# FFN up's first four steps on layer norm 1's scaled input, with mean and deviation applied to their products

## The reference

```
z = x @ w_in                                   # four token mixers and the merge gates
merged = sum_k sigmoid(gate_k) * (branch_k @ w_branch[k])
x = layer_norm(alpha * x + merged @ w_out, ln1_g, ln1_b)
gate_ff, up_ff = split(x @ w_ffn_up, 2)        # 2 x 5632 columns
x = layer_norm(alpha * x + (silu(gate_ff) * up_ff) @ w_ffn_down, ln2_g, ln2_b)

layer_norm(x) = (x - mean(x)) * rsqrt(mean((x - mean(x))**2) + 1e-5) * g + b
```

```
x @ w = ( (g*c) @ w  -  mu * (g @ w) ) / s  +  b @ w
```

## Time and profile before

| | |
|---|---|
| median of 3 runs | 1759.1 us (1758.75 to 1760.94) |
| profiled execution | 1759.97 us, span 1758.2 us |
| TensorE busy | 1710.1 us (97% of the span) |
| VectorE, ScalarE busy | 1036.0 us (59%), 791.3 us (45%) |
| mean granted TensorE clock | 0.993 |
| DMA | 329.63 MB, 187 GB/s |

### The profile page before, as it was taken

One profiled execution on the slowest core, in us unless ns is written; L12 is line 12 of the kernel. 1 busy time (PEld: TensorE's weight loads), 2 busy tenths in 40 slices (PEclk: granted clock), 3 DMA queues, 4 the chain that ended last, 5 costly groups with the idle time before them and its releaser, 6 DMA issues.

```text
span 1758.2 us, 33337 instructions
## 1 busy us (share of the span) xinstructions
PE 1710.1 (97%) x13826; PEld 1657.0 (94%) x13826; DVE 1036.0 (59%) x1218; ACT 791.3 (45%) x878; POOL 39.8 (2%) x79
## 2 busy tenths in 40 slices
PE   7999999999999999999997999999999999999995
PEld 7999989899999998999996999999999999999995
DVE  7787888656557544555587444444444444454655
ACT  5554544557444444444346444444344443333433
POOL 4000000000010000000000000000000000000000
PEclk9999999999999999999999999999999999999998
DMA  7565567776657877566553555555555555555552
GB/s 236 161 193 157 154 195 242 233 230 214 206 156 237 280 248 247 171 180 181 179 174 116 173 178 178 178 177 178 179 178 179 179 179 179 180 180 180 180 180 73
DMA packets 309119, 329.63 MB, mean 187 GB/s; under 512 B 12176, under 2 KB 289940, under 8 KB 308757
## 3 DMA queue, kind: packets, MB, share of 16 engines
q1 hardware_dynamic: 307612, 326.59, 59.4%
q10 hardware_dynamic: 1400, 1.54, 0.2%
HBM read 322.31 MB, written 5.77 MB: 187 GB/s over the span
## 4 chain that ended last, share of the span: by engine, by line
PE 93%; DVE 4%; ACT 1%; DMA 1%; issue 0%; SPq 0%; ACTq 0%; DVEq 0%
PE ps L701 15%; PE ps L1061 15%; PE ps L1060 15%; PE ps L1062 14%; PE ps L702 14%; PE ps L703 14%; PE ps L791 1%; PE ps L771 1%; PE ps L930 1%; DVE w_split L1484 1%; DMA w_in_ring<-in_w_in 1%; PE ps L750 0%; PE ps L739 0%; PE ps L717 0%; PE ps L724 0%
## 5 line engine op out<-in xcount | busy, mean ns | idle before, releaser
L2164 DVE TENSOR_TENSOR w_lo<-w_raw,w_hi 128x1024 fp32r<-128x1024 f32 x264 | 323.0, 1225 | 366.1 <-ACT w_hi L1398 364.6
L701 PE MATMUL ps<-xh,w_split 128*128 128x264 f32 x1680 | 485.7, 289 | 13.5 <-DVE w_split L1484 13.5
L1484 DVE TENSOR_TENSOR w_split<-w_in_ring,w_split 128x1024 fp32r<-128x1024 f32 x276 | 337.5, 1226 | 262.1 <-ACT w_split L1109 252.4
L1398 ACT ACTIVATE w_hi<-w_raw 128x1024 fp32r<-128x1024 f32 x264 | 279.7, 1061 | 454.4 <-PE ps L1062 449.5
L702 PE MATMUL ps<-xl,w_split 128*128 128x264 f32 x1680 | 478.7, 285 | 0.0
L703 PE MATMUL ps<-xh,w_split 128*128 128x264 f32 x1680 | 478.0, 285 | 0.0
L1109 ACT ACTIVATE w_split<-w_in_ring 128x1024 fp32r<-128x1024 f32 x276 | 290.7, 1059 | 358.4 <-DMA w_in_ring<-in_w_in 269.5
L1060 PE MATMUL ps<-xh,w_hi 128*128 128x264 f32 x1408 | 402.9, 286 | 12.8 <-DVE xl L2215 12.8
L1061 PE MATMUL ps<-xl,w_hi 128*128 128x264 f32 x1408 | 403.3, 286 | 0.0
L1062 PE MATMUL ps<-xh,w_lo 128*128 128x264 f32 x1408 | 402.6, 286 | 0.0
L701 PEld LDWEIGHTS ps<-xh,w_split 128*128 128x128 f32 x1680 | 317.9, 189 | 36.6 <-issue 25.7
(11 more groups left out here) (436 smaller groups left out, 1627.3 us busy)
## 6 DMA issues: line engine op xcount, KB each, us to landing
w_in_ring<-in_w_in SPq DMA_DIRECT2D x210, 512.0 KB, 3.7
w_raw<-in_w_ffn_up SPq DMA_DIRECT2D x176, 512.0 KB, 3.5
w_raw<-in_w_ffn_down SPq DMA_DIRECT2D x88, 512.0 KB, 3.3
kv<-in_cache_k SPq DMA_DIRECT2D x64, 258.0 KB, 3.8
w_in_ring<-in_w_branch SPq DMA_DIRECT2D x32, 512.0 KB, 3.4
kv<-in_cache_v SPq DMA_DIRECT2D x64, 256.0 KB, 3.7
w_in_ring<-in_w_out SPq DMA_DIRECT2D x32, 512.0 KB, 3.3
x_t<-in_x SPq DMA_DIRECT2D x8, 264.0 KB, 5.3
```

The lines of the kernel that those rows point to most:

```text
L701: nc.tensor.matmul(out, w_split[:, slot, 0, c], right_h[:, k, :], start=first, stop=False)
L1398: A_(w_hi[:, n % RING2, :], raw[:, n % RING2, :], ACT.Copy).then_inc(sem("hi2"), 1)
L1484: V.tensor_tensor(w_split[:, slot, 1, :], w_in_ring[:, slot, 1, :], w_split[:, slot, 0, :], ALU.subtract).then_inc(sem("lo_done"), 1)
L2164: V.tensor_tensor(w_lo[:, n % RING2, :], raw[:, n % RING2, :], w_hi[:, n % RING2, :], ALU.subtract).then_inc(sem("lo2"), 1)
```

## The change

The scaled input of the first four steps is z = g * c, c being the centred pair `xp` before mean and deviation are known. It is split into `zh` and `zl` pair by pair in the out passes, by ScalarE (`z_high`) and VectorE (`z_low`). Two columns more, gain and bias, stand beside the 264 of each tile, so that the same matmuls also give g @ w and b @ w. FFN up's steps 0 to 3 multiply by `zh` and `zl`; mean and deviation are applied by VectorE to what comes out of PSUM (`normal`), and the bias enters in `silu_z` and `h_product_z`. The sums for mean and variance are two pairs of matmuls and stand after chunk 2 of step 0. x1 is made from `xp` beside steps 1 to 3 (`X1_AT` says at which step and chunk), and split (`x1_high`, `x1_low`) at the start of step 4, which with all later steps runs on `x1h` and `x1l`. Steps 0 to 4 are written out, the loop begins at step 5. The pivot's sum is asked for two chunks earlier, squares stand one chunk later for pairs 2 to 5, the Sqrt table is no longer loaded by an instruction of its own ahead of layer norm 1.

```diff
+Z_STEPS = 4
+X1_AT = [(1, 4), (1, 5), (2, 0), (2, 1), (2, 5), (3, 0), (3, 1), (3, 5)]
...
+    XW = KT * (TOK + 2) * 4
...
+    xh = place("xh", [P, KT, TOK], F32R, at_xh + XW - XB)
+    xl = place("xl", [P, KT, TOK], F32R, at_xl + XW - XB)
+    zh = place("zh", [P, KT, TOK + 2], F32R, at_xh)
+    zl = place("zl", [P, KT, TOK + 2], F32R, at_xl)
+    x1h = place("x1h", [P, KT, TOK], F32R, at_xh)
+    x1l = place("x1l", [P, KT, TOK], F32R, at_xl)
...
-        until(last_chunk(pass_of("out", 1, 0)) + 4)
+        until(last_chunk(pass_of("out", 1, 0)) + 2)
         layer_pivot(0)
         until(END - 1)
-        layer_sums(0, xp[:, KT - 2:KT, :])
...
+        for i in range(Z_STEPS):
             for j in range(8):
+                if i == 0 and j < 4:
+                    pe.wait_ge(sem("z_low"), 2 * (j + 1))
+                up_chunk(i, j, zh, zl, TOK + 2)
+                if i == 0 and j == 2:
+                    pe.wait_ge(*told("acc_all", 1))
+                    sums("l_mu", 0, acc_d, 2)
+                    sums("l_var", 0, acc_q, 2)
+        for j in range(8):
+            if j < 4:
+                pe.wait_ge(sem("x1_low"), j + 1)
+            up_chunk(Z_STEPS, j, x1h, x1l)
+        with nc.tensor.Fori(Z_STEPS + 1, UP_STEPS) as i:
+            for j in range(8):
+                up_chunk(i, j, x1h, x1l)
...
-                if n == last_chunk(pass_of("out", m, 0)) + (12 if m == 0 else 9 if m == 1 else 5):
+                if n == last_chunk(pass_of("out", m, 0)) + (12 if m == 0 else 9 if m == 1 else 6):
                     squares(0, m, xp)
+                    z_high(m)
...
+        def z_high(m):
+            for t in (2 * m, 2 * m + 1):
+                A_(zh[:, t, 0:TOK], xp[:, t, :], ACT.Copy, scale=lnv[:, 0, t:t + 1])
+            A_(zh[:, 2 * m:2 * m + 2, TOK:TOK + 2], gain_bias(m), ACT.Copy).then_inc(sem("z_high"), 1)
...
         highs(0, 4)
         squares(0, 6, xp)
-        steps.do(A_(small[:, 63:64], ones[:, 0:1], ACT.Sqrt))
+        z_high(6)
         squares(0, 7, xp)
+        z_high(7)
+        highs(C_UP + 4, C_UP + 7)
         deviation(0)
+        highs(C_UP + 7, C_UP + 8)
...
+        def silu_z(i):
+            act.wait_ge(*told("z_gate", i + 1))
+            for t in range(2):
+                ins = A_(sg[:, t, :], sg[:, t, :], ACT.Silu, bias=small[:, 2 * t + 1:2 * t + 2])
+            ins.then_inc(sem("sg_z"), 1)
...
+        def x1_values(m):
+            act.wait_ge(*told("x1_norm", m + 1))
+            for t in (2 * m, 2 * m + 1):
+                ins = A_(x1[:, t, :], xp[:, t, :], ACT.Identity, scale=lnv[:, 0, t:t + 1], bias=lnv[:, 1, t:t + 1])
+            ins.then_inc(sem("x1_done"), 1)
+        def x1_high(k):
+            act.wait_ge(sem("x1_done"), 2 * (k + 1))
+            act.wait_ge(sem("used2"), 8 * Z_STEPS - 4 + k + 1)
+            A_(x1h[:, 4 * k:4 * k + 4, :], x1[:, 4 * k:4 * k + 4, :], ACT.Copy).then_inc(sem("x1_high"), 1)
+        for i in range(1, Z_STEPS + 1):
+            for j in range(8):
+                highs(8 * i + j, 8 * i + j + 1)
+                if j == 1:
+                    silu_z(i - 1)
+                if (i, j - 2) in X1_AT:
+                    x1_values(X1_AT.index((i, j - 2)))
+                if i == Z_STEPS and j < 4:
+                    x1_high(j)
+                if j == 5:
+                    h_high_z(i - 1)
...
+        def z_low(m):
+            dve.wait_ge(sem("z_high"), m + 1)
+            for t in (2 * m, 2 * m + 1):
+                V.scalar_tensor_tensor(zl[:, t, 0:TOK], xp[:, t, :], lnv[:, 0, t:t + 1], zh[:, t, 0:TOK], ALU.mult, ALU.subtract)
+            V.tensor_tensor(zl[:, 2 * m:2 * m + 2, TOK:TOK + 2], gain_bias(m), zh[:, 2 * m:2 * m + 2, TOK:TOK + 2],
+                            ALU.subtract).then_inc(sem("z_low"), 1)
...
+        residual(0, 7, xp)
+        squares_added(0, 6)
+        z_low(6)
         dve.wait_ge(*used(END - 2))
         lows(0, 2)
+        out_pass(0, 7, pass_of("out", 7, 0), used(END - 1), xp)
+        lows(2, 3)
+        squares_added(0, 7)
         tell(dve, "acc_all", 1)
+        z_low(7)
+        lows(3, 6)
+        dve.wait_ge(*made("l_mu", 1))
...
+        tell(dve, "variance", 1)
+        lows(6, 7)
+        dve.wait_ge(*told("l_dev", 1))
+        then(V.reciprocal(mu_r[:, 1, :], mu_r[:, 1, :]))
+        then(V.tensor_scalar(minus_r[:, 0, :], mu_r[:, 1, :], -1.0, None, ALU.mult))
+        lows(7, 8)
...
+        def normal(dst, col, p, i):
+            own = small[:, col:col + 4].rearrange("p (t c) -> p t c", c=2)
+            dve.wait_ge(sem("used2"), i * 8 + 4 * (p - pg) + 4)
+            then(V.tensor_copy(own, PS[:, BANK(p):BANK(p) + 2, TOK:TOK + 2]))
+            do(V.scalar_tensor_tensor(dst[:, 0, :], mu_r[:, 0, :], small[:, col:col + 1], PS[:, BANK(p), 0:TOK],
+                                      ALU.mult, ALU.subtract))
+            V.scalar_tensor_tensor(dst[:, 1, :], mu_r[:, 0, :], small[:, col + 2:col + 3], PS[:, BANK(p) + 1, 0:TOK],
+                                   ALU.mult, ALU.subtract).then_inc(sem(f"evac{p % 2}"), 1)
+            steps.settle()
+            dve.wait_ge(sem(f"evac{p % 2}"), i + p // 2 + 1)
+            then(V.tensor_tensor(dst[:, :, :], dst[:, :, :], minus_r[:, :, :].to_broadcast([P, 2, TOK]), ALU.mult))
+        def gate_z(i):
+            normal(sg, 0, pg, i)
+            tell(dve, "z_gate", 1)
+        def h_product_z(i):
+            if i:
+                dve.wait_ge(sem("hl_done"), i)
+            normal(hx, 4, pu, i)
+            dve.wait_ge(sem("sg_z"), i + 1)
+            for t in range(2):
+                do(V.scalar_tensor_tensor(hx[:, t, :], hx[:, t, :], small[:, 5 + 2 * t:6 + 2 * t], sg[:, t, :], ALU.add, ALU.mult))
+            steps.settle()
+            tell(dve, "hx_z", 1)
...
+        gate_z(0)
+        for i in range(1, Z_STEPS + 1):
+            for j in range(8):
+                lows(8 * i + j, 8 * i + j + 1)
+                if j == 2:
+                    h_product_z(i - 1)
+                if j == 6:
+                    h_low_z(i - 1)
+                if (i, j) in X1_AT:
+                    x1_norm(X1_AT.index((i, j)))
+                if i == Z_STEPS and j < 4:
+                    x1_low(j)
+            if i < Z_STEPS:
+                gate_z(i)
```

More of the change, by code:

```diff
@@ L1042, in layer_sums, with products @@
             ins.then_inc(sem("made"), 1)
-        until(last_chunk(pass_of("out", 1, 0)) + 4)
+        until(last_chunk(pass_of("out", 1, 0)) + 2)
         layer_pivot(0)
         until(END - 1)
-        layer_sums(0, xp[:, KT - 2:KT, :])
-        def products(slot, bank, right_h, right_l, k0, first, last, part=None):
+        def products(slot, bank, right_h, right_l, k0, first, last, width=TOK):
             for kk in range(CK):
-                if part:
-                    pe.wait_ge(*part(k0 + kk))
                 rh, rl = right_h[:, k0 + kk, :], right_l[:, k0 + kk, :]
                 for half in range(2):
-                    out = PS[:, bank + half, 0:TOK]
+                    out = PS[:, bank + half, 0:width]
                     c = slice((kk * 2 + half) * P, (kk * 2 + half) * P + P)
@@ L1063, in products, with up_chunk @@
             ins.then_inc(sem("used2"), 1)
-        def up(i, part=None):
-            for j in range(8):
[L1067 to L1075, removed]
+        def up_chunk(i, j, right_h, right_l, width=TOK):
+            n, p, kc = C_UP + j, P_UP + j // 4, j % 4
+            if kc == 0:
+                pe.wait_ge(sem(f"evac{p % 2}"), i + p // 2)
+            pe.wait_ge(sem("lo2"), i * 8 + (n + 1))
+            products(n % RING2, BANK(p), right_h, right_l, CK * kc, kc == 0, kc == 3, width)
+        for i in range(Z_STEPS):
+            for j in range(8):
+                if i == 0 and j < 4:
[12 more added lines that the diff above has]
+                up_chunk(i, j, x1h, x1l)
         for m in range(8):
@@ L1530, in due @@
                     centre(0, 1, xp)
-                if m < 6 and n == last + (13 if m == 0 else 10 if m == 1 else 7):
+                if m < 6 and n == last + (13 if m == 0 else 10 if m == 1 else 8):
                     squares_added(0, m)
+                    z_low(m)
+        def z_low(m):
[4 more added lines that the diff above has]
+                            ALU.subtract).then_inc(sem("z_low"), 1)
         def residual(n, m, dst):
             pair = slice(2 * m, 2 * m + 2)
+            high, low = ((xh, xl), (x1h, x1l))[n]
             if m >= PIVOT[n]:
-                then(V.scalar_tensor_tensor(dst[:, pair, :], xl[:, pair, :], ALPHA, pivot[:, :, :].to_broadcast([P, 2, TOK]),
+                then(V.scalar_tensor_tensor(dst[:, pair, :], low[:, pair, :], ALPHA, pivot[:, :, :].to_broadcast([P, 2, TOK]),
                                             ALU.mult, ALU.subtract))
             else:
-                then(V.tensor_scalar(dst[:, pair, :], xl[:, pair, :], ALPHA, None, ALU.mult))
```

(28 more changed lines are left out.)

64 lines of the change are left out of this document (28 added, 36 removed).

## The result

The changed kernel takes 1736.63 us in the median of four runs (1736.06 to 1737.95), the kernel before on the same chips 1760.02 (1758.75 to 1762.63, four runs): ratio 0.9866, 95% interval 0.9855 to 0.9878.

A forecast was written before the change was run, and what follows sets the result against it. TensorE, busy 97% of the span, was taken to bound the kernel; 19.24 + 0.24 - 0.7 = 18.8 us off the profiled 1759.97 gave 1741.2, as a median 1740.3 (chance 0.72), range 1738.3 to 1748.

The forecast's parts named there:

- The hole: TensorE's layer norm 1 stall between out passes and FFN up's second step, put at 23.6 us; shortening it gains 19.24 us.
- the walk: Timeline after the change, from the out passes' end: TensorE waits 2.6 us before chunk 0, step 1 starts at 966.45.
- The out passes: Asking for the pivot's sum earlier removes VectorE's 4.2 us idle, pays for three `z_low`, and gains TensorE's 0.24 us wait.
- The two columns: FFN up steps 0 to 3: 768 matmuls of 266 columns for 264 cost 0.7 us; ends 0 and 75 us.
- VectorE in steps 1 to 4 and x1: VectorE at most 87% busy, x1 ready with 1.5 us slack: no cost; rival of VectorE falling behind 4 to 10 us, chance 0.11.
- Instructions, DMA, LN 2: Same weight loads and order, steps 1 to 4 written out, layer norm 2's sequence kept; nothing added to the sum.
- The range: Forecast kernel time of 1738.3 to 1748 us, taking in the half clock and most of VectorE falling behind.
- The half clock: Rival: TensorE's clock falls after the new wait before chunk 0, costing 2.4 us, so 1742.7; chance 0.10.
- The slow z matmuls: Rival, chunks 0 to 31: 1064-byte row starts slow 768 matmuls; from 25 ns each slower than before; chance 0.05.
- late for step 4: Rival: x1 isn't ready at step 4, so the stall only moves there, no gain, time 1759; chance 0.02.

## Why the prediction was wrong

- *The hole.* Forecast 19.24 us less 0.18 for step 0's columns, 19.1. Measured: 9.83 in the gap and 9.29 in step 0, 19.1. The mechanism was right: the wait ahead of chunk 0 is there with the releaser forecast, and the norm's chain is hidden, chunk 7's low half ending at 955.4, 6.3 us ahead of its chunk. That the sizes agree so closely is luck. The prediction took 985.69 for the first matmul of step 1 in the kernel before; it is the third (line 1062 comes last of the three of `products`). The first matmuls of steps 0 and 1 before are

```profile
950.56 0.56 PE L1060 MATMUL ps<-xh,w_hi 128*128 128x264 f32 x1 [6.13 <-DVE xl L2215]
...
985.45 0.28 PE L1060 MATMUL ps<-xh,w_hi 128*128 128x264 f32 x1
```

So the hole was 23.4 us and not 23.6, and the gain by the walk 19.0. What was 0.24 too much there came back elsewhere: the gap to chunk 0 is 2.3 us where the walk had 2.7 (a wait of 2.0 for 2.6), and step 0 took 0.1 us longer than walked.

- *The out passes.* 0.24 forecast, 0.22 measured. The reason given, that the idle time pays for `z_low`, does not hold: with the sum late there is one wait of 0.24 us and nothing for `z_low`.
- *The two columns.* 0.7 us forecast over four steps, 0.24 x 4 = 0.96 measured against the old pitch. But the old pitch was the wrong base: against the step of the same kernel it is 0.45 x 4 = 1.8, of which the matmuls alone, at this offset, put more than half on the row stride. The prediction had the stride as an unknown, 75 us at worst.
- *VectorE in steps 1 to 4 and x1.* Right: TensorE waits nowhere there, and the fullest step, step 1, has 20.0 us of VectorE's work where 20.4 at most were forecast.
- *The step that failed* is "Instructions, DMA, LN 2", which put steps 4 to 21 and all that is unedited at nothing because loads, order and sequences are the same. Their operands are not at the same addresses. The diff says so (`XW` in `at_xl`, `x1l` for `xl`), and I read it as layout without a price. It was worth 3.8 us in steps 4 to 21, shown by both runs that move the offset and nothing of the algorithm. Ahead of the out passes the gaps give 1.6 us (121.87 to 121.54 ns over some 4900 matmuls). The 1.4 us of the table fit that but don't prove it, since profiles with one and the same layout differ by over 1 us in that stage (841.0 to 842.2).
- *The range* had no bound for it. The trace of before had a hint: FFN up and out passes at 2.94 us a chunk, FFN down with 2.92, for the same 24 matmuls. A difference between stages of one instruction is a cost with an unknown cause, and what moves tiles can move it.
- *Rivals.* The half clock did not come (1.00 in each window above). The slow z matmuls did in part, with 2.1 ns of the 25 that would have turned the sign. x1 was not late for step 4: its window has 23.31 us, as a loop step.

## What to carry to other kernels

Where the matmul's pitch bounds the kernel, the addresses of its operands are an input of the time, here 0.4% of it for one offset of 128 bytes: if a change shifts a region, compare the pitch in stages that it does not edit before any gain or loss is put down to the edit. A layout found by measuring matmuls alone at 64 places carried over to the kernel in sign, in two of three stages also in size, and cost no instruction. A chain as long as a layer norm can be taken off the path by putting its scalars behind the product, if the order on the splitting engine lets the first weights through before the last of the activations.

## What the runs showed of the hardware

- Float32r matmuls (the type of the high and low halves) of 264 columns follow at 120.6 to 122.6 ns at full clock, depending on where the low input lies against the high one and the low weights against the high ones, modulo 256 bytes. Rows 1280 bytes apart, all at one place modulo 256, gave 120.0, but this is no rule: with 256 columns in rows 1024 bytes apart one place gave 119.9, the low input 128 bytes off it 117.8. In the loop the gaps repeat from step to step, within 1 ns in the kernel before and 3 ns in the kernel before with the offset, one by one between 115 and 132 ns. Why is open.
- At one stride and offset a column more costs 0.3 ns (272 words) to 0.5 ns (264 words). In the rows of the table with 117.9, 121.5 and 125.0 ns the 256, 264 and 272 columns take each some 11 to 12 ns more than columns at 2.4 GHz. The Trainium skill's page TensorE: Matmul & The Clock Gate, section "Wait — 56ns, not 53.3ns?", has 2.5 ns for that fixed part; the measurements here decide for this kind of matmul.
- A pause of TensorE of 2.0 us left its granted clock at 1.00 (936.87 to 964.66 above).
